# Hybrid decoder layer: q, k and v of the next head pair projected between the attention steps of this one, a plain first tile pair, and four more gate tiles in the block-product stage

## What is computed

```
h = RMSNorm(x)
[cB, cC, cH, q, k, v, gA, gB] = h @ w_in        # 512 x6, then 1024 x2 columns
yA = (cB * dwconv3_causal(cC * cH)) @ w_a
beta[t,s] = sigmoid(q_t.k_s/sqrt(64) + b_h), s < t strictly          # 8 heads x 64
A[t,s] = beta[t,s] * prod_{s<j<t}(1-beta[t,j])
yB = (sum_s A[t,s] v_s) @ w_b
x += RMSNorm((sigmoid(gA)*yA + sigmoid(gB)*yB) @ w_o)
... ConvFFN, per-layer embedding gate (untouched)
```

## Time and profile before

| | |
|---|---|
| median of 3 runs | 1721.18 us (1719.48 to 1724.46) |
| the profiled execution: its time, its span | 1719.32 us, 1717.6 us |
| mean granted TensorE clock | 0.993 |
| PE busy, share of the span | 1657.8 us, 97% |
| DVE, ACT, POOL busy | 1184.6, 832.3, 360.6 us |

### The profile page before, as it was taken

The page is one execution under the profiler, slowest core; times in us unless marked ns, Lnnn a source line. Parts: engine busy times, 40 slices in busy tenths (PEclk is TensorE's granted clock), DMA queues, the critical chain, the costliest instruction groups (busy, mean ns, idle before and its releaser), DMA issues.

```text
span 1717.6 us, 25950 instructions
## 1 busy us (share of the span) xinstructions
PE 1657.8 (97%) x8709; PEld 1416.9 (82%) x8709; DVE 1184.6 (69%) x1678; ACT 832.3 (48%) x1433; POOL 360.6 (21%) x291
## 2 busy tenths in 40 slices
PE   9699988999989989999999999999999999999998
PEld 8588887787887977998878888888888888888886
DVE  7965525537447257655878888888888798777566
ACT  7322235546456366214554444444444544465665
POOL 1144300000000000000116666666666100000100
PEclk9899999999999999999999999999999999999999
DMA  5112253131131221435222222222221863244333
GB/s 167 45 56 76 84 155 95 34 107 58 51 113 36 80 80 69 141 131 185 99 87 78 77 77 77 77 77 77 77 77 40 277 237 116 82 147 168 120 130 117
DMA packets 178314, 174.98 MB, mean 102 GB/s; under 512 B 17423, under 2 KB 144235, under 8 KB 178220
## 3 DMA queue, kind: packets, MB, share of 16 engines
q1 hardware_dynamic: 167274, 168.87, 30.3%
q10 hardware_dynamic: 10946, 4.91, 1.0%
HBM read 131.89 MB, written 41.84 MB: 101 GB/s over the span
## 4 chain that ended last, share of the span: by engine, by line
PE 61%; DVE 2%; issue 0%; ACT 0%; DMA 0%; POOL 0%; SPq 0%; DVEq 0%; POOLq 0%; ACTq 0%
PE pair L3595 10%; PE pair L3655 8%; PE pair L3656 8%; PE pair L3657 8%; PE pair L3793 4%; PE pair L3795 4%; PE pair L3794 4%; PE pair L3664 2%; PE pair L3116 2%; PE pair L3093 2%; PE pair L3091 2%; PE pair L3092 2%; PE pair L3603 1%; DVE left L2511 1%; PE pair L3779 1%; PE pair L3778 1%
## 5 line engine op out<-in xcount | busy, mean ns | idle before, releaser
L3164 PE MATMUL pair<-xh,wh 128*128 128x384 f32 (+1 forms) x600 | 209.0, 348 | 4.8 <-DVE qs L2451 4.5
L3166 PE MATMUL pair<-xh,wl 128*128 128x384 f32 (+1 forms) x600 | 197.3, 329 | 0.0
L3165 PE MATMUL pair<-xl,wh 128*128 128x384 f32 (+1 forms) x600 | 197.0, 328 | 0.0
L1195 POOL TENSOR_TENSOR hn<-hn 128x512 f32<-128x512 f32 x4 | 5.2, 1288 | 654.8 <-DVE hn L2645 654.8
L3164 PEld LDWEIGHTS pair<-xh,wh 128*128 128x128 f32 x600 | 114.2, 190 | 9.2 <-DVE qs L2451 4.8
L3793 PE MATMUL pair<-woph,foph 128*128 128x512 f32 x308 | 120.4, 391 | 0.0
L3795 PE MATMUL pair<-woph,fopl 128*128 128x512 f32 x308 | 119.9, 389 | 0.0
L3794 PE MATMUL pair<-wopl,foph 128*128 128x512 f32 x308 | 119.9, 389 | 0.0
L3165 PEld LDWEIGHTS pair<-xl,wh 128*128 128x128 f32 x600 | 114.3, 191 | 0.0
L3166 PEld LDWEIGHTS pair<-xh,wl 128*128 128x128 f32 x600 | 113.7, 189 | 0.0
L2195 DVE TENSOR_TENSOR wl<-raw,wh 128x1024 fp32r<-128x1024 f32 x33 | 40.4, 1224 | 70.9 <-ACT wh L1349 70.7
(11 more groups left out here) (529 smaller groups left out, 4847.8 us busy)
## 6 DMA issues: line engine op xcount, KB each, us to landing
rawp<-in_w_up SPq DMA_DIRECT2D x88, 256.0 KB, 3.8
wd<-in_w_down SPq DMA_DIRECT2D x55, 256.0 KB, 3.0
raw<-in_w_in SPq DMA_DIRECT2D x52, 256.0 KB, 3.4
f_spill<-cv SPq DMA_DIRECT2D x22, 552.0 KB, 2.8
f<-f_spill SPq DMA_DIRECT2D x44, 256.0 KB, 5.6
gat<-gate_spill SPq DMA_DIRECT2D x16, 544.0 KB, 4.4
x_spill<-x SPq DMA_DIRECT2D x16, 512.0 KB, 3.2
wraw<-in_w_in SPq DMA_DIRECT2D x28, 256.0 KB, 3.9
```

The source lines that it names most:

```text
L3164: t_.matmul(b, h, xhi, start=(k == 0), stop=False, skip_group_check=True)
L3165: t_.matmul(b, h, xlo, start=False, stop=False, skip_group_check=True)
L3166: ins = t_.matmul(b, l, xhi, start=False, stop=(k == KD - 1), skip_group_check=True)
```

## The change

- `WIDE_PAIRS` has nine pairs. Eight gate tiles are made in the block-product stage (`WIDE_GATES` = 8), eight in the turns (`TURN_GATES` = 1, 1, 1, 5).
- The first pair is plain (`wide_plain`, order "abScd", four products of 24 matmuls of 512 columns). DVE no longer makes the sums of weight blocks for it.
- Only the first turn's q, k and v are made ahead of its slots. Those of turn c+1, with one gate tile, are the filling of turn c's slots (96 pieces; the last turn has 120 pieces of five gate tiles). The first 17 slots take twice as many pieces as the others (`EARLY, WEIGHTS`).
- The cached keys of turn c+1 are turned in slots 18, 20, 25 and 26 of turn c (`PAST_AT`), and their scores are made in slots 25 and 27.
- q, k, v buffers are double. They take the place of `cout` and `oT`, so the attention output goes out to `o_spill` and comes back with `cout` in the last turn.

The diff, cut to its core:

```diff
-def first_piece(n):
-    return n * IN_FILL * KD // SLOTS
+TURN_GATES = (1, 1, 1, 5)
+EARLY, WEIGHTS = 17, (2, 1)
+def first_piece(c, n):
+    done = [WEIGHTS[0] * min(m, EARLY) + WEIGHTS[1] * max(m - EARLY, 0) for m in (n, SLOTS)]
+    return done[0] * len(jobs_of(c)) * NG * KD // done[1]
+PAST_AT = {18: 0, 20: 1, 25: 2, 26: 3}
-WIDE_PAIRS = [("g", 0), ("c", 1), ("b", 0), ("c", 2), ("c", 3), ("b", 2), ("g", 1)]
+WIDE_PAIRS = [("g", 0), ("c", 1), ("b", 0), ("c", 2), ("g", 1), ("c", 3), ("b", 2), ("g", 2), ("g", 3)]
-    return "1S267543" if n == 0 else "162S7543"
+    return "162S7543" if n else "abScd"
...
+            for c in range(NC4):
+                gates = 0
+                for j in range(TURN_JOB[c], TURN_JOB[c + 1]):
+                    kind, m = JOBS[j]
+                    if j + 3 < IN_JOBS + 2:
+                        load(in_job(j + 3) if j + 3 < IN_JOBS else ab_job(j + 3 - IN_JOBS))
+                    if kind == "q":
+                        hold(p_past, 4 * m)
+                        keys(m, 0)
+                        keys(m, 1)
+                    if kind == "g" and gates == 0 and c + 1 < NC4:
+                        hold(p_x, 4 * (c + 1))
+                        for q in range(4):
+                            values(c + 1, q)
+                    if kind == "g" and gates == TURN_GATES[c] - 1 and c + 1 < NC4:
+                        hold(p_past, 4 * (c + 1) + 1)
+                        keys(c + 1, 2)
+                        hold(p_past, 4 * (c + 1) + 2)
+                        keys(c + 1, 3)
...
-            block_sums()
             wide_h(0, 0)
             wide_h(0, 1)
...
+            def wide_plain():
+                for i, what in enumerate(wide_order(0)):
+                    if what == "S":
+                        wide_sample(0)
+                        continue
+                    h, half = divmod("abcd".index(what), 2)
+                    pe.wait_ge(d_wl, W_LOW[f"h{h}", 0])
+                    if what == "d":
+                        wide_fold(0)
...
+                    if c + 1 < NC4:
+                        if n == 25:
+                            pages(c + 1, 0)
+                        if n in PAST_AT:
+                            past(c + 1, PAST_AT[n])
+                        if n == SLOTS - 1:
+                            pages(c + 1, 1)
+                            new_keys(c + 1)
```

More of the change, by code:

```diff
@@ new lines, in v_copy, with gate, k_twice @@
+            def v_copy(j, gr):
+                s_.activation(part(vT[:, :], gr), unit_in(j, gr), ACT.Copy).then_inc(a_kv, 1)
+            def gate(j, gr):
+                b = unit_in(j, gr)
+                act.wait_ge(stg_out[gr], stn[gr].at())
+                s_.activation(stg[gr][:, 0:GROUPS[gr][1]], b, ACT.Sigmoid).then_inc(a_gt, 1)
+                stn[gr].step(16)
+            def k_twice(c):
+                act.wait_ge(a_qk, 1 + 2 * NG * (c + 1))
+                for h in range(2):
+                    s_.activation(ks2[c % 2][h][other(h), 0:SEQ], f(ks2[c % 2][h])[own(h), 0:SEQ], ACT.Copy)
@@ new lines, in sample_in @@
+            def sample_in(c):
+                act.wait_ge(p_xt, xn_.step())
+                src = xb_[:, 0:P].rearrange("p (b h q) -> p b h q", b=NB, h=2)
+                dst = ot[:, CW:CW + NS] if c + 1 < NC4 else oT[:, c, SEQ:TOK]
+                for h in range(2):
+                    rows = slice(64 * h, 64 * h + 64)
+                    ins = s_.activation(dst[rows, :].rearrange("p (b q) -> p b q", q=NT), src[rows, :, h, :], ACT.Copy)
+                ins.then_inc(a_x, 1)
+                if c + 1 < NC4:
+                    act.wait_ge(a_x, xn_.at(1))
+                    act.dma_start(o_spill[c:c + 1, :, SEQ:TOK].rearrange("o p t -> p (o t)"), dst).then_inc(o_out, 16)
@@ new lines, in _, with unit_in, rest @@
+            for t in kl:
+                for h in range(2):
+                    v.memset(f(t[h])[other(h), :], 0.0)
+            def unit_in(j, gr):
+                dve.wait_ge(p_unit, NG * j + gr + 1)
+                return banks[(NG * j + gr) % 2][:, 0:GROUPS[gr][1]]
+            def rest(lo, j, hi, gr, end=TOK):
+                b = unit_in(j, gr)
+                for h in range(2):
+                    o, w = GROUPS[gr][0], min(GROUPS[gr][1], end - GROUPS[gr][0])
+                    ins = v.tensor_tensor(lo(h)[:, o:o + w], b[own(h), 0:w], f(hi[h])[own(h), o:o + w], ALU.subtract)
+                ins.then_inc(d_qk, 1)
@@ L2474, in pair, with k_low, biases @@
+            def k_low(c, j, gr):
+                dve.wait_ge(a_qk, 1 + qkn.step())
+                if gr == NG - 1:
+                    v.tensor_copy(ks[:, :], unit_in(j, gr)[:, SEQ - GROUPS[gr][0]:]).then_inc(d_qbd, 1)
+                rest(lambda h: kl[c % 2][h][own(h), :], j, ks2[c % 2], gr, SEQ)
+            def biases(c):
                 if c == 0:
```

734 lines of the change are left out of this document (385 added, 349 removed).

## The result

The changed kernel took 1766.97 us (median of 4 runs, 1764.87 to 1769.45), the one before 1720.62 us: a ratio of 1.0268, 95% interval 1.0251 to 1.0284. It is slower, as forecast, but by 46 us and not by 25, and lies above the range. The profiled execution took 1769.45 us, with a span of 1767.7.

What follows compares the result with a forecast made beforehand. It took TensorE, busy 97% of the span, to bound the kernel. Its terms, -1.0 + 42.8 - 47.2 - 6.1 - 13 + 49.2 = +24.7 us on the profiled 1719.3, gave 1744 us, slower; range 1715 to 1763 (likeliest case 1732 to 1756).

Steps and rivals of the forecast that it cites:

- Step 1: Opening pair made plain: no wait for block sums, but the second pair waits for `wadl` until 79.0; -1.0 us.
- Step 2: Block-product stage: two more pairs at 21.4 us each, with gaps like the pairs beside them; +42.8 us.
- Steps 3 and 4: Four gate tiles fewer in the turns, -47.2 us; first turn's projections lose a stall and its slow clock, -6.1 us.
- Step 5: Attention slots of the four turns: TensorE's idle time falls from 28 to 14.5 us; -13 us.
- Step 6: End of the first three turns: TensorE waits for pages of k issued behind v's, 16.4 us each; +49.2 us.
- The first rival: Turns' page loads stay hidden, TensorE finds its keys in slot 25: 1695 us, chance 0.13.
- the second: Page loads half as dear, 0.7 us an issue, waits of 8 us per turn: about 1720 us, chance 0.09.
- The third: DVE becomes the bound in the slots through q's and k's subtractions, +18 us over three turns: 1762 us, chance 0.12.

Runs made afterwards that it cites:

- e9: Changed kernel with six edits of queue order, pages of k first among them, and the turn's gate tile put out between halves of v's pages: 1688.06 us.
- l1: e9 without the edit of e3, so the ninth pair's load is late again: 1694.84 us.
- e3: Changed kernel with the ninth pair's load issued ahead of the last b pair's stores, the wait for them and the first load of q: 1764.48 us.
- e4: Changed kernel with ACT copying k's rows ahead of slot 11's sigmoids in three turns: 1762.33 us.
- l2: e9 without the edit of e4, so k's rows are copied behind the sigmoids again: 1694.30 us.
- e5: Changed kernel with the next projection's weights loaded ahead of the sixteen pages of v in the first turn: 1764.91 us.
- l3: e9 without the edit of e5, so the first turn's load stands behind v's pages again: 1690.62 us.
- e6: Changed kernel with the last turn's first gate tile put out ahead of the seven loads of cout and oT: 1763.34 us.
- e1: Changed kernel with the last eight pages of k of a turn issued ahead of the sixteen pages of v: 1716.70 us.
- e2: Changed kernel with v's pages at constant cache places, without the register load, in the second to fourth turn (sample output differs): 1740.71 us.
- l4: e9 without the edit of e6, so the loads of cout and oT stand ahead of the store again: 1698.91 us.
- e10: e9 with the opening reordered so the second pair's high and low weights are made ahead of the last sums': 1685.02 us.

## Why the prediction was off

The direction, the mechanism and its place were right, and the size was not. The span was to be 1717.6 + 24.7 = 1742.3 and is 1767.7: 25.4 over.

**Step 1, the opening pair (-1.0): right.** The second pair starts at 79.5 for 79.0, behind a wait of 4.0 us for `wadl`, with the lower clock after it. The wait of 5.0 for the samples' sums, ahead of it, wasn't seen; it moved nothing, since VectorE made `wadl` only at 78.22.

**Step 2, two more pairs (+42.8): the price right, the stage not.** 21.6 us a pair in e9. But "where TensorE has 0.8 us of gaps" carried the absence of waits over to a queue whose order I hadn't followed: with nine pairs, the last load stands behind the stores and the first load of q. That is +6.3 (l1) to +8.6 (e3).

**Steps 3 and 4 (-47.2, -6.1): right.** The first turn's projections take 42.5 for 42.4. Without the unforeseen waits (e9) the first three turns take what the prices give without pages, within 1.2 us, and the last 3 less.

**Step 5, the slots' idle time (-13): this step failed.** It is nearly right for the chain of sigmoid, scan and product: `beta` waits fall from 15.4 to 11.3, where "below 10" was forecast, and 3.5 of them are the late load. It priced idle time by engine loads alone and followed neither ACT's nor SP's own order. Three waits are outside it: k's rows behind the sigmoids (7.2 to 7.8 over three turns, e4 and l2), the load behind sixteen values' pages in the first turn (3.9 to 5.6, e5 and l3), and the gate tile's store behind `cout` and `oT` in the last (5.4, e6), of which I had written that they "cost nothing: seven DMAs early in the last turn, whose first reader is in slot 25". Their readers weren't the question; the store behind them was.

**Step 6, the pages of k (+49.2): right mechanism, 13% small.** The waits are 15.8, 16.0 and 16.3 us for 16.4. Taken out (e1) the three turns give 56.5: 53.1 for the two batches' lateness, where I had 14 + 2.4 a turn and it is 14.9 + 2.8, and 3.4 besides, of which half clock at 410.42 (1.1) and at 453.06 (1.6) makes 2.7. Issue time rules: e2 shows it one for one. The first rival, hidden pages, and the second have no support left. The third, DVE as the bound, named the time nearest to the measured one, 1762, and would have been right by luck: with the waits gone the turns take 87.5 us, not more.

These parts (56.5 - 49.2 for the pages, then the ninth pair's load, k's rows, the first turn's load and the store) add to 7.3 + 7 + 7.5 + 4.5 + 5.4 = 32 us, more than the 25.4 missed; they are priced in different kernels, and l4 shows that they are not independent. What each costs in the changed kernel alone is known to some 3 us only. The rule of the Trainium skill that was set against step 6 ("DMA: Bandwidth & Descriptors", section "Issuing engines are not separate DMA queues") would have given the first rival's 1695 us; for a DMA whose place is read into a register first, the runs decide against it: 1.08 us of issuing for 1.8 to landing, and 50 us of time.

## What to carry to other kernels

Where work moves into a stage, follow each hand-ordered queue through it (SP's issues, ACT's copies) and ask of every entry what now stands ahead of it; the balance of engine loads finds none of these waits. Issue first what is needed first: here the pages of k alone turned 2.7% lost into 0.2% won, and all eight edits of order together (e10) made it 2.3% won, with the same work. And price small waits in a kernel without large ones: under the page stalls four edits measured 2 to 5 us each, with runs 3 to 15 us apart, while put back into the clean kernel they measured 3 to 11, with runs 3 to 5 apart.

## What the hardware showed

A DMA at an address that is first loaded into a register took 1.08 us of SP's time (16 in 17.36 us), at a constant address 0.48 (16 in 7.63 us). Filling the page stalls with dummy matmuls kept the granted clock at full level through the two middle turns and raised its mean from 0.977 to 0.989, and the kernel took no less time (1769.95 us for 1766.97): in the second turn the stretch at 0.50, from 514.9 to between 518 and 519, lay in front of a wait for a page that landed at 519.32. A wait of 1.98 us was followed by the lower clock in the second turn of the changed kernel, and not in its third turn or in e1's second.
